# A gate/up projection unit with its bank copy, its weight sums and its silu in another order

## The reference, cut to what matters

```python
gu = h @ w_gate_up            # 512 x 2048 by 2048 x 11264
g, u = gu[..., :D_FF], gu[..., D_FF:]      # D_FF = 5632
return (jax.nn.silu(g) * u) @ w_down
```

## Time and profile before

| what | value |
|---|---|
| median of 3 runs | 1776.37 us (1775.12 to 1778.19) |
| the profiled execution's own time | 1779.96 us |
| its span (first to last instruction) | 1778.2 us |
| granted TensorE clock, mean | 0.993 |
| PE busy | 1734.9 us, 98% |
| DVE busy | 1293.9 us, 73% (68 of 81 us in the stage of the units) |
| ACT busy | 778.3 us, 44% |
| POOL busy | 102.0 us, 6% |
| stage of the 41 units | about 507 to 1331 us |

### The profile page before, as it was taken

How to read it: one execution, slowest core, us unless ns; L and a number is a source line. 1 busy time by engine, 2 the same in 40 slices (tenths; PEclk the granted TensorE clock), 3 DMA queues, 4 the chain that set the end, 5 groups by cost and what they waited for, 6 DMA issues and landing times.

```text
span 1778.2 us, 24615 instructions
## 1 busy us (share of the span) xinstructions
PE 1734.9 (98%) x8928; PEld 1475.8 (83%) x8928; DVE 1293.9 (73%) x1367; ACT 778.3 (44%) x944; POOL 102.0 (6%) x130
## 2 busy tenths in 40 slices
PE   8999999999999999999999999999998999999997
PEld 6888888888888888888888888888887788888885
DVE  6432333335888888888888888888889888888885
ACT  5232322235444444544445444454444344434354
POOL 3000000003000000000000000000000000000044
PEclk9999999999999999999999999999999999999998
DMA  7333332262233444434443344434458886877854
GB/s 228 81 95 85 80 91 74 71 213 73 71 119 119 129 154 142 119 118 135 137 129 118 118 146 147 132 118 125 138 178 247 239 244 168 226 210 206 245 136 127
DMA packets 294748, 254.67 MB, mean 143 GB/s; under 512 B 8112, under 2 KB 257200, under 8 KB 288432
## 3 DMA queue, kind: packets, MB, share of 16 engines
q1 hardware_dynamic: 288848, 224.71, 41.6%
q0 software_dynamic: 3456, 23.07, 6.6%
q10 hardware_dynamic: 2400, 6.29, 1.0%
HBM read 203.72 MB, written 27.26 MB: 130 GB/s over the span
## 4 chain that ended last, share of the span: by engine, by line
PE 69%; DVE 12%; issue 10%; ACT 7%; DMA 1%; POOL 1%; ACTq 0%; DVEq 0%; POOLq 0%
PE ps L1753 22%; PE ps L2018 21%; PE ps L1967 15%; PE ps L1973 7%; DVE raw L1460 5%; ACT split L1031 5%; DVE split L1449 3%; PE ps L1951 2%; ACT ps L1053 1%; DMA operand_raw<-a_sums 1%; PE ps L1956 1%; DVE tmp L1269 1%; DVE xres L1611 1%; PE ps L1766 0%; DVE hT L1257 0%
## 5 line engine op out<-in xcount | busy, mean ns | idle before, releaser
L1031 ACT ACTIVATE split<-raw 128x1024 fp32r<-128x1024 f32 x295 | 312.0, 1058 | 367.0 <-DVE raw L1460 157.1
L1449 DVE TENSOR_TENSOR split<-raw,split 128x1024 fp32r<-128x1024 f32 x295 | 360.2, 1221 | 92.6 <-ACT split L1031 88.2
L2018 PE MATMUL ps<-split,operand_hi 128*128 128x512 f32 x1232 | 384.2, 392 | 9.4 <-DVE xres L1611 5.0
L1753 PE MATMUL ps<-hT,split 128*128 128x512 f32 (+1 forms) x1392 | 288.6, 368 | 0.8 <-DVE split L1250 0.8
L2018 PEld LDWEIGHTS ps<-split,operand_hi 128*128 128x128 f32 x1232 | 232.6, 189 | 62.0 <-ACT split L1120 4.8
L1753 PEld LDWEIGHTS ps<-hT,split 128*128 128x128 f32 x1392 | 241.3, 189 | 43.5 <-issue 1.0
L1967 PE MATMUL ps<-hT,split 128*128 128x512 f32 x984 | 246.4, 392 | 0.0
L1120 ACT ACTIVATE split<-down_slot 128x2048 fp32r<-128x2048 f32 (+1 forms) x84 | 148.3, 1772 | 218.6 <-DVE down_slot L1596 106.3
L2018 PE MATMUL ps<-split,operand_lo 128*128 128x512 f32 x616 | 240.9, 391 | 0.0
L1967 PEld LDWEIGHTS ps<-hT,split 128*128 128x128 f32 x984 | 177.0, 189 | 31.7
L1460 DVE TENSOR_TENSOR raw<-raw 128x1024 f32<-128x1024 f32 x164 | 199.8, 1218 | 0.1
(11 more groups left out here) (161 smaller groups left out, 1716.6 us busy)
## 6 DMA issues: line engine op xcount, KB each, us to landing
raw<-in_ffn_w_gate_up_dram SPq DMA_DIRECT2D x172, 512.0 KB, 4.8
down_slot<-in_ffn_w_down_dram SPq DMA_DIRECT2D x40, 1024.0 KB, 7.7
raw<-in_fox_w_in_dram SPq DMA_DIRECT2D x24, 1024.0 KB, 5.8
a_sums<-pack SPq DMA_DIRECT2D x22, 1024.0 KB, 6.2
down_slot<-down_slot POOLq DMA_DIRECT2D x20, 1024.0 KB, 7.4
operand_raw<-a_sums SPq DMA_DIRECT2D x35, 512.0 KB, 5.1
raw<-in_fox_w_out_dram SPq DMA_DIRECT2D x8, 1024.0 KB, 5.1
xres<-in_x_dram SPq DMA_DIRECT2D x4, 1024.0 KB, 8.2
```

The source lines that it names most:

```text
L1031: nc.scalar.activation(ring(r, 0, n), source, ACT.Copy).then_inc(t_hi, 1)
L1449: nc.vector.tensor_tensor(ring(r, 1, n), source, f32(ring(r, 0, n)), ALU.subtract).then_inc(t_lo, 1)
L1753: ins = nc.tensor.matmul(bank, stationary(sp, t), moving(mp, t), start=first and t == tiles[0] and (sp, mp) == PASSES[0], stop=last and t ...
L2018: ins = nc.tensor.matmul(banks[:, tile, :], operand[e][part][:, i, tile * P:(tile + 1) * P], down_ring(dn, part_of_t, e)[:, i * BANK:(i + ...
```

## The change

On ScalarE, a unit's list begins after it with the left half of the unit before (`take_gate_before`, split off from `gate_before`) and `copy_first`; only then come the rounding for product 2 (`sum_hi(at, 2)`) and silu (`gate_before`). Before, the order was: left half, silu, rounding for product 2, `copy_first`. The two copies gain a wait each for combinations of the unit before (`combined`).

On VectorE, three things change places: `second_sum` now comes directly after remainder 1, ahead of `gate_right_before`; remainder 2 comes ahead of `act_before`; and at the end of a unit `first_sum` of the next unit comes directly after remainder 0 of that unit, ahead of the last `add_right`. No operation is added or removed, and no buffer changes.

```diff
 def copy_first(at):
     act.wait_ge(product, at.product(0))
     if at.r is None:
         act.wait_ge(a_done, PLAIN)
+    else:
+        act.wait_ge(combined, at.combined(-5))
 def copy_second(at):
     act.wait_ge(product, at.product(1))
+    if at.r is not None:
+        act.wait_ge(combined, at.combined(-2))
-def gate_before(at):
+def take_gate_before(at):
     act.wait_ge(product, at.product(-1))
     take_left(ga[:, HALF:S], bank_before(at))
+
+def gate_before(at):
+
     act.wait_ge(combined, at.combined(0))
     nc.scalar.activation(ga[:], ga[:], ACT.Silu).then_inc(silu_done, 1)
 # ScalarE, unit
     if at.r is not None:
+        take_gate_before(at)
+        copy_first(at)
+    sum_hi(at, 2)
+    if at.r is not None:
         gate_before(at)
-    sum_hi(at, 2)
-    copy_first(at)
-    if at.r is None:
+    else:
+        copy_first(at)
         copy_plain(2, third)
     plain_hi(at.r, at.first + 3, "B21", at.u)
 # VectorE, unit
     unit_lo(at, 1)
+    second_sum(at)
     if at.r is not None:
         gate_right_before(at)
-    second_sum(at)
-    if at.r is not None:
+        unit_lo(at, 2)
         act_before(at)
     else:
         plain_out(2, third)
         ...
-    unit_lo(at, 2)
+        unit_lo(at, 2)
 ...
     if not end:
         unit_lo(at.next(), 0)
+        first_sum(at.next())
     dve.wait_ge(x_taken, at.taken(2))
     add_right(cc[:, 0:HALF], bank_of(at, 2))
     if end:
         ...
-    else:
-        first_sum(at.next())
 # ScalarE, behind the last unit
+take_gate_before(LAST_UNIT.next())
 gate_before(LAST_UNIT.next())
```

## The result

The changed kernel takes 1765.41 us (median of 4 runs, 1764.15 to 1766.71); the kernel before took 1777.28 us beside it (median of 4, 1775.12 to 1779.61). The ratio is 0.9933, 95% interval 0.9916 to 0.9950: 11.9 us less (8.9 to 14.9 by the interval), where 11.9 was worked out (1764.5). The profiled execution took 1764.64 us, its span is 1762.8.

The account below looks back on a forecast made before the run. TensorE, busy 78.77 of 80 us, was taken to bound the kernel. Loop gain 11.3 plus 0.6 at the end, 11.9, took the profiled 1779.96 to 1768.1, as a median 1764.5 us; range 1755 to 1771.5.

Parts of the forecast that it names:

- (1): ScalarE's copy: starts about 3.0 us behind product 0, ends at 3.6, leaves TensorE's path and gives back 20.9 us.
- (2): ScalarE's list behind the copy: silu ends at about 5.6, ahead of the multiplication needing it at 6.1; costs nothing.
- (3): VectorE's sums and remainders up to remainder 2: waited sums follow after 1.25 us, not 1.13; remainder 2 starts at 4.99.
- kind A: Units with three packed differences, 20 of 40, 18 in the loop: lose 0.47 us at product 3, take 20.0.
- kind B: Units with a single packed difference: remainder 3 handed over 0.26 us ahead of need, no stall, unit takes 19.55.
- The rival that hung on the rule: VectorE's waited sums cost nothing, following remainders after 1.13 us: gain 16.6, 1759.8 us; chance 0.14.
- (4): VectorE between remainders 2 and 3: activations now ahead make remainder 3 0.87 us later; product 3 loses 0.47 in kind A.
- (5): Load of the next B22: ends at 14.5, wanted 8 us after issue, slowest load 7.5 us; costs nothing.
- the edit does nothing: At product 2, the copy still ends the wait, held by something other than its place; no separate chance given.
- The whole gain: VectorE's remainder 3 isn't late, steps after rounding 1 taking 0.6 us less: all 20.9 gained, 1755.5 us; chance 0.12.
- Kind B stalls too: At product 3, a longer VectorE chain stalls single-difference units also: gain 7.0 at the upper bound, 1769.4 us; chance 0.14.
- Slower: VectorE's list between remainders 1 and 3 takes at least 0.60 us longer; at 1 us longer, 1794 us; chance 0.10.

Follow-up runs that it names:

- The kernel with the late differences: The changed kernel with the packed differences moved behind the combination that product 4 waits for, the multiplication staying: 1755.27 us, ratio 0.9868 to the kernel before.
- each half alone: Two kernels against the kernel before: only ScalarE's list in the new order, 1807.25 us, ratio 1.0162; only VectorE's list in the new order, 1801.31 us, ratio 1.0125.

## Why the prediction was right

(1) *The copy.* It starts at 886.14, 3.07 behind product 0; 3.0 was given. Its wait is gone in all 40 units, as predicted.

(2) *ScalarE's list.* Rounding 2 starts at 3.90, as given, and nothing on ScalarE is late. VectorE's idle time ahead of remainder 2 is 0.80, where about 1.0 was given.

(3) *VectorE's front.* In kind A it came out right in sum because two errors cancel, which is luck. `first_sum` follows its remainder after 1.26 (1.25 given), but `second_sum` after 1.35, 0.10 more. The handoff from the second sum to rounding 2 took 0.03 (885.71 + 1.23 to 886.97) where I took 0.16 from the earlier trace rows. In kind B both sums of a loop unit follow after 1.35. The code written out behind the loop tells the two parts of that price: there every one of these sums follows after 1.26, as in this unit (u = 0):

```profile
1240.72 1.22 DVE L1460 TENSOR_TENSOR split<-raw,split 128x1024 fp32r<-128x1024 f32 x1 [0.93 <-ACT split L1031]
1241.98 1.22 DVE L1471 TENSOR_TENSOR raw<-raw 128x1024 f32<-128x1024 f32 x1
```

So a sum that waits for the remainder directly ahead pays 0.12 over the 1.14 of an unwaited operation everywhere, and some 0.09 more in places, all of them in the loop. The rule of the Trainium skill that I had set beside it ("VectorE: DVE Perf Modes", "The DRAIN you can't avoid": a semaphore between two operations costs nothing) doesn't hold here: 1.26 and 1.35 with the wait, 1.14 without. The same section adds, and my prediction left it out, that a next operation that isn't held starts earlier; the 1.14 behind an operation 1.23 long agrees with that. The rival that hung on the rule is out.

(4) *VectorE's middle.* Remainder 3 was to start at 9.23 and started at 9.25 (892.32). The wait that it makes, 0.47 by my sum, is 0.40, because TensorE took the low part up 0.05 behind its end and not 0.12; this was my lower bound. Kind B kept its lead and takes 19.55: its remainder 3 starts at 8.42 (911.44, product 0 at 903.02) where 8.39 was given. That too is a sum of errors that cancel: 0.2 more for the two sums, 0.13 less for the handoff, and the single difference is followed after 0.34 and not 0.42. In the written-out units 0.23 was given for kind A, and 0.32 and 0.24 came.

The step that was missing is one that pulls the other way. In the loop's first unit, u = 0, product 3 loses 0.60 and not 0.40, so the unit takes 20.17, where 20.0 was given for all of kind A. The chain of waits shows where: remainders 1 and 2 start 0.12 behind their roundings, not 0.03, with the queue's own wait instruction of line 1459 in between.

```profile
923.91 0.04 issue
923.95 1.24 DVE split L1460
925.19 0.03 issue
925.22 0.05 DVEq L356
925.26 0.05 issue
925.31 1.24 DVE raw L1471
926.55 0.02 issue
926.57 1.07 ACT split L1031
927.64 0.03 issue
927.67 0.04 DVEq L1459
927.71 0.04 issue
927.75 0.07 DVE split L1460
```

Two such handoffs make 0.18 of the 0.20 per iteration. My rows of the loop come from units u = 2 and 3, and I had taken them for all.

*The sum.* The kernel with the late differences has no wait in the stage, 798.87 us, and serves as the zero. Before, the waits were 820.52 - 798.87 = 21.7 (20.9 given: u = 0 lost 0.65, not 0.55). After, they are 808.56 - 798.87 = 9.7 (9.0 given: 9 x 0.20 more for u = 0, 18 x 0.07 less for the handoff of (4), some more in the first iteration). Both terms were 0.7 to 0.8 too small, so that their difference was hit more closely than either is luck, and more closely than the interval of the runs can tell. What was right is the mechanism, the place of the new wait and the kinds of unit that have it.

(5) *The loads.* The slowest load took 8.2 us after the change (7.5 before), more than the 8 us that I had counted for B22. Still no wait on a load appears in the stage, and `second_sum`, which needs B22, follows remainder 1 after 1.34 to 1.36 in all 36 loop units, so B22 was never late.

The rivals: *the edit does nothing* is out, since the waits on the copy are gone. *The whole gain* did not come with this order; it came (1755.27) with the differences moved behind the combination. *Kind B stalls too* did not happen in the changed kernel and was made to happen with 0.68 more in front of remainder 3. *Slower* happened for each half alone, at other places than the one I had named: in product 2.

## What to carry to other kernels

When an instruction is late, look at what stands in front of it in its own engine's list, and try to move only that first: one copy moved by one place gained 21 us, where a reordering of two engines, which also freed it, gained 12. When a step is put ahead of others, work out when each consumer behind them is due; VectorE at 84% had room for everything, and still three small operations in the wrong place cost TensorE 0.4 to 0.6 us each time. A move that shifts a step on which the other engine's list waits needs the other list moved with it: silu waits for an addition of VectorE and the multiplication waits for silu, and here each half alone lost 23 to 29 us. The copy moved by one place shifted neither, and needed nothing on VectorE.

## What the runs showed of the hardware that I had not expected

The time from a sum on VectorE to the rounding on ScalarE that waits for it was 0.16 us in one place and 0.03 us in another of the same kernel, with the same three waits ahead of it. The chain of waits shows two of them as steps of ScalarE's queue in the slow case (before rounding 1: lines 1029 and 1030) and none in the fast one. Likewise a remainder follows its rounding after 0.12 instead of 0.03 in the first unit of each loop iteration (line 1459 in the chain), and in the loop the second sum starts 0.12 instead of 0.03 behind the end of its remainder (line 356 in the chain). All of these longer times lie in the loop, whose waits compare with register values. In the code written out behind it, where they compare with constants, each of the three starts 0.03 to 0.04 behind the operation that it waits for. Whether the register values are the reason, and why some places of the loop are spared, no run here settles.
